# Splitting P and V into two parts each for their product, in a three-block transformer kernel on one NeuronCore

## The reference, cut to what matters

```python
q, k, v, gate_a, u_b, gate_b, q_idx, k_idx, w_idx, merge = split(rms_norm(x) @ w_in)
score = sum_h relu(q_idx_h . k_idx) * w_idx_h          # 8 index heads of 64
sel   = top_k(where(visible, score, -1e30), 256)       # per query
attn  = softmax(q . k[sel] / 8) @ v[sel]               # 8 heads of 64, one K and one V for all heads
y_a   = (attn * silu(gate_a)) @ w_a
y_b   = (multiscale_pool(u_b) * silu(gate_b)) @ w_b
x     = x + (sig(merge_a) * y_a + sig(merge_b) * y_b) @ w_out
```

## Time and profile before

| | us |
|---|---|
| median of 3 runs (3599.98 to 3604.37) | 3604.36 |
| the profiled execution | 3597.27 |
| its span | 3595.4 |
| TensorE (PE) busy in it | 3357.2 |
| VectorE (DVE) busy | 1806.4 |
| ScalarE (ACT) busy | 1261.4 |
| GpSimd (POOL) busy | 1212.1 |

### The profile page before, as it was taken

The page is one execution under the profiler, slowest core; times in us unless marked ns, Lnnn a source line. Parts: engine busy times, 40 slices in busy tenths (PEclk is TensorE's granted clock), DMA queues, the critical chain, the costliest instruction groups (busy, mean ns, idle before and its releaser), DMA issues. The chain is left out here.

```text
span 3595.4 us, 45087 instructions
## 1 busy us (share of the span) xinstructions
PE 3357.2 (93%) x18148; PEld 2932.0 (82%) x18148; DVE 1806.4 (50%) x3015; ACT 1261.4 (35%) x1894; POOL 1212.1 (34%) x835
## 2 busy tenths in 40 slices
PE   5899999998998999999898999998899899999997
PEld 4788999998888899999875788876777588888885
DVE  4578999653356799975424144433433411000014
ACT  4553212452265422135314344344522522222223
POOL 3324633215332363311434432311253432323331
PEclk8999999999999999999998999999999999999998
DMA  5101122204310112210322411111242111111111
GB/s 139 33 24 42 57 81 90 76 1 160 101 54 24 36 51 78 93 72 1 124 90 82 127 40 35 40 47 48 71 141 94 30 47 47 47 47 49 46 52 48
DMA packets 284175, 230.59 MB, mean 64 GB/s; under 512 B 31473, under 2 KB 257408, under 8 KB 283584
## 3 DMA queue, kind: packets, MB, share of 16 engines
q1 hardware_dynamic: 253792, 116.40, 12.0%
q0 software_dynamic: 23264, 85.89, 6.8%
q10 hardware_dynamic: 6912, 25.41, 1.8%
HBM read 177.29 MB, written 52.36 MB: 64 GB/s over the span
## 5 line engine op out<-in xcount | busy, mean ns | idle before, releaser
L548 PE MATMUL big<-H,wsp 128*128 128x348 f32 (+2 forms) x9792 | 1916.6, 355 | 70.6 <-POOL H L1605 33.9
L548 PEld LDWEIGHTS big<-H,wsp 128*128 128x128 f32 (+1 forms) x9792 | 1684.7, 190 | 271.8 <-issue 35.5
L1605 POOL TENSOR_TENSOR wsp<-raw,wsp 128x1024 fp32r<-128x1024 f32 (+2 forms) x246 | 544.0, 2211 | 1488.2 <-ACT wsp L1071 1478.1
L548 PE MATMUL big<-SP,wsp 128*128 128x512 f32 x1920 | 451.0, 395 | 0.0
L548 PEld LDWEIGHTS big<-SP,wsp 128*128 128x128 f32 x1920 | 359.1, 187 | 90.4 <-issue 1.7
L1071 ACT ACTIVATE wsp<-raw 128x1024 fp32r<-128x1024 f32 (+2 forms) x246 | 238.4, 969 | 509.0 <-PE big L548 372.0
L2263 DVE MAX8 top<-SC 128x8 f32<-128x272 f32 (+6 forms) x448 | 367.9, 821 | 0.0
L2269 DVE MATCH_REPLACE8 SC<-top,SC 128x272 f32<-128x272 f32 (+6 forms) x448 | 364.5, 814 | 0.0
L2422 DVE TENSOR_TENSOR X<-X,big 128x1024 f32<-128x1024 f32 (+1 forms) x26 | 29.6, 1139 | 476.1 <-PE big L548 475.9
L1119 ACT ACTIVATE rows_a<-rows_a,head_min 128x1040 f32<-128x1040 f32 (+8 forms) x130 | 101.9, 784 | 128.1 <-DVE head_min L2041 127.9
L697 PE MATMUL small<-V,PT_a 128*128 128x64 f32 x1152 | 146.4, 272 | 0.1
(11 more groups left out here) (268 smaller groups left out, 3828.3 us busy)
## 6 DMA issues: line engine op xcount, KB each, us to landing
raw<-in_w_in SPq DMA_DIRECT2D x108, 512.0 KB, 3.9
raw<-in_w_ff SPq DMA_DIRECT2D x64, 512.0 KB, 4.1
raw<-in_w_out SPq DMA_DIRECT2D x24, 512.0 KB, 5.3
gate_b_scratch<-tm POOLq DMA_DIRECT2D x16, 522.0 KB, 3.1
gate_a_scratch<-tm ACTq DMA_DIRECT2D x16, 522.0 KB, 2.9
tm<-gate_a_scratch POOLq DMA_DIRECT2D x16, 522.0 KB, 3.8
tm<-gate_b_scratch POOLq DMA_DIRECT2D x16, 522.0 KB, 4.6
tm<-xT_scratch POOLq DMA_DIRECT2D x16, 522.0 KB, 5.2
```

Of the source, the lines that this page charges most:

```text
L548: mm = pe.matmul(dst(o, width), w[wp][:, k, 0:cols], rhs(xp, k)[:, t0:t0 + width], start=(k == 0 and i == 0), stop=(k == rows - 1 and i == 2))
L1605: pool.tensor_tensor(dst, src, hi.bitcast(F32), ALU.subtract).then_inc(*S.inc(name, *key))
```

## The change

1. In all attentions P (after the turn) and V become two float32r parts. `move_hi`: ScalarE copies every turned tile from PSUM to the high part; `move_lo`: VectorE subtracts the high part from PSUM and writes the low part. A tile's product with V is now three float32r matmuls of 64 columns: P high by V high, P high by V low, P low by V high.
2. The tiles of a unit are turned into two banks used by turns (`tiles_a`, `tiles_b`): units of more than 4 tiles use both, smaller ones one of the two. TensorE's order in step k is now scores(k), turn(k-2), values(k-3). ScalarE's is move_hi(k-2), exponential(k-1), and in the second layer the work between comes last. VectorE's is mask(k), move_lo(k-2).
3. V's low part is made by VectorE after ScalarE's copy, and only then is V ready: in the first layers before the index stage, in the neighbourhood attention in step 3 (`values_lo`).
4. The rows of the first attentions lie in three rows of `tm` (`row_a`), no more in two buffers of their own; a row's maker waits for the turn three units back. The last 16 keys of block 7 are no longer apart; the logits of 576 keys lie in one stretch over two banks.
5. The silu gates are loaded per block (`load_silu`) into `silu_a`, 128 columns of four rows.
6. In the second of the first layers the unit of the meta queries (block -1) is left out (`LAST_A`); its result is not part of the output.
7. The index queries cover 896 columns (blocks 1 to 7): projection and rotation in two pieces of 448, copies and products over 896 columns.

```diff
+        QI_COLS = slice(META + P, META + SEQ)
+        QI_PIECE = (SEQ - P) // 2
+        pieces_qi = [(i * BANK, META + P + i * QI_PIECE, QI_PIECE) for i in range(2)]
...
+        LAST_A = [-1] * (DEPTH - 1) + [0]
...
+        def tiles_a(u, k):
+            if u["tiles"] > 4:
+                return [(0, 0, 4), (1, 4, u["tiles"] - 4)]
+            return [(k % 2, 0, u["tiles"])]
+        def row_a(k):
+            return tm[:, (2, 3, 0)[k % 3], 0:1040]
+        def tiles_b(u, k):
+            if len(u["kts"]) > 4:
+                return [(0, 0, 3), (1, 3, len(u["kts"]) - 3)]
+            return [(k % 2, 0, len(u["kts"]))]
...
                 def values(k):
-                    for kt in range(u["tiles"]):
-                        mm = pe.matmul(out[:, u["h"] * HD:(u["h"] + 1) * HD], PT_a[:, k % 2, kt, :], V[:, kt, :],
-                                       start=(u["h"] == 0 and kt == 0), stop=False, skip_group_check=True)
+                    for name, of, parts in (("moved_hi", 0, (0, 1)), ("moved_lo", 1, (0,))):
+                        for i, (_, first, count) in enumerate(tiles_a(u, k)):
+                            pe.wait_ge(*S.at(name, *u["key"], i))
+                            for kt in range(first, first + count):
+                                for part in parts:
+                                    mm = pe.matmul(out, PT_a[:, k % 2, of, kt, :], V[:, part, kt, :],
+                                                   start=first_of_bank, stop=False, skip_group_check=True)
...
+                    if 3 <= k < N:
+                        scores(k)
                     if 2 <= k < N + 2:
                         turn(k - 2)
-                    if 3 <= k < N:
-                        scores(k)
...
+        def move_hi(act, u, k, tiles, PT, before):
+            for i, (bank, first, count) in enumerate(tiles(u, k)):
+                act.wait_ge(*S.at("turned", *u["key"], i))
+                if before is not None:
+                    act.wait_ge(*S.at("weighted", *before))
+                act.activation(PT[:, k % 2, 0, first:first + count, :], turned_tiles(bank, count), ACT.Copy)\
+                    .then_inc(*S.inc("moved_hi", *u["key"], i))
+        def move_lo(dve, u, k, tiles, PT, before):
+            for i, (bank, first, count) in enumerate(tiles(u, k)):
+                dve.wait_ge(*S.at("moved_hi", *u["key"], i))
+                if before is not None:
+                    dve.wait_ge(*S.at("weighted", *before))
+                dve.tensor_tensor(PT[:, k % 2, 1, first:first + count, :], turned_tiles(bank, count),
+                                  PT[:, k % 2, 0, first:first + count, :].bitcast(F32), ALU.subtract)\
+                    .then_inc(*S.inc("moved_lo", *u["key"], i))
...
         def act_attention(act, units, between):
             for k in range(N + 5):
-                if between:
-                    between(k)
                 if 2 <= k < N + 2:
-                    move(act, units[k - 2], (k - 2) % 2, "act")
-                if k < N:
-                    u, at = units[k], column_b(units[k])
+                    move_hi(act, units[k - 2], k - 2, tiles_b, PT_b, weighted_before(units, k - 2))
+                if 1 <= k < N + 1:
+                    u, at = units[k - 1], column_b(units[k - 1])
...
+                between(k)
...
+            def values_lo(what, c):
+                wait(("v_part", what, c))
+                dve.tensor_tensor(V2[:, 1, :, :], ps2(psum_of[("v", what, c)]).rearrange("p (k d) -> p k d", k=NQ),
+                                  V2[:, 0, :, :].bitcast(F32), ALU.subtract).then_inc(*S.inc("v_ready", what, c))
```

More of the change, by code:

```diff
@@ L603, in values @@
                 def values(k):
                     u = units[k]
-                    for e in moved_events(u):
-                        pe.wait_ge(*S.at(*e))
                     if opens_b(u) and earlier_b(block_b(u)):
                         pe.wait_ge(*S.at("gated", *earlier_b(block_b(u))))
[L609 to L613, removed]
+                    out = small[slot_b(u)][:, column_b(u) * HD:(column_b(u) + 1) * HD]
@@ new lines, in values @@
+                    n, total = 0, 3 * len(u["kts"])
+                    for name, of, parts in (("moved_hi", 0, (0, 1)), ("moved_lo", 1, (0,))):
+                        for i, (_, first, count) in enumerate(tiles_b(u, k)):
+                            pe.wait_ge(*S.at(name, *u["key"], i))
+                            for kt, rows, v in u["kts"][first:first + count]:
+                                for part in parts:
+                                    mm = pe.matmul(out, PT_b[0:rows, k % 2, of, kt, :], v[:, part, :],
+                                                   start=(opens_b(u) and n == 0), stop=(closes_b(u) and n == total - 1),
+                                                   skip_group_check=True)
+                                    n += 1
@@ L742, in attention_a @@
                         turn_back(units[k - 6]["j"])
[L744 to L747, removed]
-                    mm = pe.matmul(big[0][:, 0:META], meta_q[:, :], KK[:, part, 0:META],
-                                   start=(part == 0), stop=(part == 1))
-                mm.then_inc(*S.inc("logits", "a", l, -1))
-                pe.wait_ge(*S.at("exped", "a", l, -1))
@@ L1125, in split_out, with exped @@
                     .then_inc(*S.inc("attn_hi", l, j))
-            for k in range(N + 8):
+            def exped(k):
+                u = units[k]
+                j, h = u["j"], u["h"]
+                if h == 0 and before_a(j, 2) is not None:
+                    act.wait_ge(*S.at("normed_out", "a", l, before_a(j, 2)))
+                exponent(u["key"], row_a(k)[:, 0:u["n"]], head_min[:, slot_a(j), h:h + 1], head_sum[:, slot_a(j), h:h + 1])
+            exped(0)
+            exped(1)
+            for k in range(2, N + 9):
```

373 lines of the change are left out of this document (174 added, 199 removed).

## The result

The changed kernel takes 3891.0 us (median of 4, 3877.8 to 3905.2) against 3603.6 (3600.0 to 3604.4): ratio 1.080, 95% interval 1.0759 to 1.0842. The direction was forecast, the size was not: +287 us for +124, outside the range. The profiled execution took 3877.8 us, with a mean granted clock of 0.928 over the span, against 0.973.

A forecast was written before the change was run, and what follows sets the result against it. TensorE, busy 93% of the span, was taken as the bound. First attentions +53.8, +6 and -3, neighbourhood +60, window +22, index queries with V's low part -14.4 made +124 on 3597.3: forecast 3725 us, range 3675 to 3770.

The forecast's parts named there:

- Price of a narrow product: All attentions: a 64-column float32r matmul costs 0.112 us, so a tile 0.335, 0.112 more; blocks 7 to 3 +53.8 us.
- (b): Rival: a narrow matmul costs its lower bound, 0.082 us, a tile 0.246; +45 us in all, 3650; chance 0.08.
- (c): Rival: weights load behind and a narrow matmul costs 0.03 us; the kernel gets faster, -29, 3575 us; chance 0.06.
- Waits of 3 to 4 us cost speed afterwards too: Neighbourhood chunk starts: matmuls just after the waits run slower, some 1.5 us a chunk, +6 in all (0 to 12).
- Starts of neighbourhood chunks: V's bias and copy come last in their step, so its turn and first product wait: +5.4 us a chunk, +21.6.
- Blocks 2 to 0: First attentions' small blocks: the new order makes a loop of turn, high copy, exponential; +3 us a layer, +6.
- Window attention: A 3-tile unit's loop takes 1.9 us: +5.3 a chunk in chunks 0 to 2, last +6, together +22 (8 to 35).
- Index queries: Projections on 896 columns save 14 us and rotations 2, all gained by the selection that follows (-8 to -18).
- V's low part: Ahead of the first layers' index stages: a subtraction of 512 and a signal, +0.8 us a layer, +1.6.
- Cover of ACT and DVE: Block 7 units of the first attentions: PE 4.7 us, ACT 2.6, DVE 2.3, so TensorE stays the bound.
- (d): Rival: ACT and DVE end last everywhere, 0.3 us more on each second-layer and small-block unit; 3775 us; chance 0.09.
- meta unit's -3: End of the first attentions: leaving out the meta unit lets the branch product start earlier, -3 us.

The follow-up runs named there:

- e8: Kernel before the change with only the index queries' part (896 columns, two pieces) added: 3584.2 us, ratio 0.9954.
- e12: Changed kernel with one float32 product a tile, V's beside-work ahead of P's moves in the neighbourhood attention, V's low part not made: 3613.7 us.
- e6: Changed kernel with one float32 product a tile in all attentions, and neighbourhood beside-work and V's low part ahead of P's moves: 3649.9 us.
- e10: Changed kernel without the P low by V high product (two narrow products a tile), neighbourhood beside-work and V's low part ahead of P's moves: 3746.3 us.
- e4: Changed kernel with ScalarE's beside-work and V's low part ahead of P's moves in the neighbourhood attention, three narrow products kept: 3887.7 us.
- e3: Changed kernel with each product of P and V streaming 128 columns instead of 64, same loads, waits and count; not the reference's attention: 3783.9 us.
- e13: Changed kernel with one float32 product a tile, neighbourhood beside-work ahead of P's moves, neither V's nor P's low part made: 3611.8 us.
- e9: Kernel before the change with the index queries' part added and the last layer's meta unit left out: 3584.5 us, ratio 0.9948.
- e5: Changed kernel with one float32 product a tile in all attentions instead of three narrow ones, order of the change kept: 3691.6 us.
- e11: Changed kernel with only P high by V high (one narrow product a tile), V's low part still made: 3626.7 us.

## Why the prediction was wrong

Differences of medians, each of one step, add up to the result: index part -19 (e8 over before), then +30 (e12 over e8: float32 products, but ScalarE doing all high moves, rows and gates moved, the new order), +36 (e6 over e12: V's low part and the waits that it makes), +96 (e10 over e6: two narrow products for one float32 one, same loads), +141 (e4 over e10: the third product), +3 (after over e4: V last; within the runs' spread).

- **Price of a narrow product: right.** Block 6 takes 33.9 us for 33.3. From e10 to after it gains 6.59 us by 56 third products, 0.118 us each for the 0.112. Blocks 7 to 3 of layer 0 gained 25.5 us for the 26.9 forecast, partly by luck: block 7 gained 3.5 for 7.2, the other four 22.0 for 19.7. Rivals (b), with 0.082, and (c), with 0.03 (about what 64 columns alone come to by the earlier trace rows), fall. By the forecast price the third product costs 1040 x 0.112 = 116 us of the 141; the rest is put down to its part of the clock.
- **The step that failed: "Waits of 3 to 4 us cost speed afterwards too ... some 1.5 a chunk, +6 (0 to 12)".** The speed isn't lost for a few instructions. It was gone for 60 us a chunk: the chunks took 29 us each over the forecast, 117 in all, where this term had 1.5 each. I read what a wait does to the clock from a place where long streams of 512 columns follow it, and put it on one where 64-column products follow. And the sum had no term for a clock that falls without a long wait, which e4 shows. The busy column doesn't show the fall: e4's window has 57.70 us busy of 57.70 at 0.50.
- **Starts of neighbourhood chunks: right in mechanism and size.** Waits of 2.5 and 3.6 us for 0.45 and 0.47 before, so 5.1 us more, forecast as 5.4.
- **Blocks 2 to 0: mis-sized.** +13 and +10 us a layer for +3. Blocks 2 and 1 gave +3.1 and +2.0 in layer 0. The new loop is dearer than I made it, for e12 with float32 products has +2.3 and +1.7, and in its blocks 2 to 0 TensorE waits ten times, 3.0 us in all, for ScalarE's exponential. Block 0 gave +8.0 there (22.1 for 14.1) and +4.7 in layer 1, mostly by the clock (0.52 and 0.63 in the windows above): e3's block 0 in layer 0, with the same count of matmuls at full clock, takes 16.2 us, and e6's 16.6.
- **Window attention: mis-sized.** A chunk takes 5 to 9 us more for the 5.3 forecast, and the last one's units run at half clock for 51 us (window below): from its first mask to its last product the stage takes 267.5 us for 230.8, +37 for +22. Of these, 12 are there in e12 too, with float32 products.
```profile
2839.30:2890.50 51.20, 49.12 (x213) 47.07 (x214) 21.53 (x53) 24.53 (x58) 23.21 (x18) 0.50 0.29 91
```
- **Index queries: right**, -16 forecast, -19 measured (-11 to -22). **V's low part: wrong**, 0.8 us a layer forecast; the waits of PE after the change have it at 5.6 us in each layer:
```profile
PE big L559 <- DVE V L2229: 11.1, 2, 5.6
```
In e12, without it, the stages ahead of the two first attentions are 9 us shorter, and the four neighbourhood chunks 28: 6 of these are waits for V, the rest the clock behind them.
- **Cover of ACT and DVE: right for DVE, in part for ACT.** P's low part costs VectorE time and the kernel none (e13). After the change TensorE is the busy engine in the half-clock stretches (60.26 of 60.30 us), so rival (d) isn't what made the loss; but its mechanism is there in small, in the 12 us of the window attention. The meta unit's -3 isn't there: e9.

Shown: with count, loads, order and the waits at a chunk's start the same, twice the columns bring the clock back sooner (mean of a chunk 0.88 in e3, 0.73 after), and so does one float32 product in place of two float32r ones (0.94 in e6, 0.70 in e10); with float32 products shorter waits do too (0.94 in e6, 0.87 in e5; 0.98 in e12, 0.94 in e6). Only argued: that both work by the array's streaming time, and not by something else. The clock also varies where nothing was changed: layer 0's block 0 takes 16.6 us at 0.89 in e6 and 15.7 at 1.00 in e12, with the same instructions; so a difference of 1 us in a block means nothing.

The two profiled executions of e12 and e8 are 26 us apart: 12 us of it lie in the window attention, 3 in the neighbourhood chunks and 7 in the first attentions. How much is ScalarE's loop and how much the order is open; e12's blocks 2 to 0 take 15.2, 12.8 and 15.7 us, before 13.0, 11.1 and 14.1.

## What to carry to other kernels

Price a narrow matmul by its weight load (in block 6, after and e3, the loads are busy 32.4 of 33.9 us, and a product of 64 columns costs what one of 128 does), and then look at the granted clock: here a row of matmuls with few columns each, busy for the whole window by the profile, ran at 0.50 for 57.7 us (e4), and everything between them too. Splitting a 64-column float32 product in three float32r ones costs half again by count and, here, as much again by the clock (e4 is 238 us over e6, about 116 of them by the count). If it must be split, streaming more columns behind each load is worth a trial (two parts or two heads side by side); e3 shows the gain in the clock (0.88 for 0.73 in a chunk), but no kernel here does that and keeps the attention's result. With float32 products a wait in front of such a stretch cost two to four times itself here: from e5 to e6 3.6 us less of waits (6.0 to 2.4) made a chunk 8 to 14 us shorter. With the narrow products the same 3.6 us less brought nothing (e4).

## What the runs showed of the hardware

- A float32r matmul of 128 columns behind its own load costs what one of 64 does: block 6 takes 33.92 us with the wide ones and 33.88 with the narrow, at full clock.
- Half clock for 57.7 us with the engine busy in all of it (e4), in a mix of 64-column float32r products, transposes and scores. With one float32 product in place of two such products, and the same loads, the mean clock of a chunk was 0.94 for 0.70 (e6, e10).
- Fewer products alone didn't cure it: one product a tile, with more waits than e4 (e11), left the clock at 0.75 to 0.91 in a chunk and at 0.50 over 15.3 us of layer 0's block 0, where PE is busy 11.4 of them.
